# Eight stick-breaking heads placed beside the query and value tiles, and three orders of VectorE instructions changed, in a sixteen-sublayer network on one core

## The reference, cut to what matters

```python
def _swiglu(x, w_gu, w_down):                       # ffn: x + 0.5 * _swiglu(rms_norm(x))
    g, u = jnp.split(x @ w_gu, 2, axis=-1)
    return (silu(g) * u) @ w_down

def _mla_mixer(h, ...):                             # latent attention, 16 heads
    c = h @ w_in                                    # 768 query latents, 256 key-value latents, 32 rotary
    q = (rms_norm(c_q) @ w_uq); kv = (rms_norm(c_kv) @ w_ukv)
    k = concat(k_nope, k_rope); q = rms_norm(q); k = rms_norm(k)   # per head, then rotary embedding
    return softmax_attention(q, k, v) @ w_out

def rg_lru_block(x, ...):                           # linear recurrence, width 1024
    y_br = gelu(y part of x @ w_in); x_br = causal_depthwise_conv(x part)
    gates = sigmoid(x_br @ w_gates + b_gates)       # gate_i, gate_r, block by block
    a = exp(-8 * gate_r * softplus(-a_param)); u = sqrt(1 - a * a) * gate_i * x_br
    h[t] = a[t] * h[t - 1] + u[t]
    return (h * y_br) @ w_out + b_out

def stick_breaking_attention(q, k, v):              # 8 heads of 128, causal
    z = q @ k.T * 128 ** -0.5
    log_1m = where(k_pos < q_pos, log_sigmoid(-z), 0)
    suffix = reverse_cumsum(log_1m) - log_1m        # along the keys
    w = where(k_pos < q_pos, exp(log_sigmoid(z) + suffix), 0)
    return w @ v
```

## Time and profile before

| | |
|---|---|
| runs of the kernel before | 2902.45 us median (2902.28 to 2902.95, 3 runs) |
| the profiled execution's own time | 2902.22 us |
| its span, first to last instruction | 2900.4 us |
| granted TensorE clock over the span | 0.993 of full speed |
| TensorE busy | 97% of the span |
| VectorE, ScalarE, GpSimd busy | 67%, 50%, 3% |
| stick-breaking sublayer | about 2557.5 to 2685.3 us of the span |

### The profile page before, as it was taken

One profiled execution on the slowest core, in us unless ns is written; L12 is line 12 of the kernel. 1 busy time (PEld: TensorE's weight loads), 2 busy tenths in 40 slices (PEclk: granted clock), 3 DMA queues, 4 the chain that ended last, 5 costly groups with the idle time before them and its releaser, 6 DMA issues.

```text
span 2900.4 us, 47103 instructions
## 1 busy us (share of the span) xinstructions
PE 2809.0 (97%) x19844; PEld 2616.1 (90%) x19844; DVE 1955.2 (67%) x2547; ACT 1439.2 (50%) x1970; POOL 96.0 (3%) x147
## 2 busy tenths in 40 slices
PE   8999989999998999999999999999999999998998
PEld 8999979999996999998889999998899889987997
DVE  5757876565665656557655665588665778756877
ACT  5445554444456444445644444555544644445543
POOL 0000000000012000001100000000000100000000
PEclk9999999999999999999999999999999999999999
DMA  7654436676551665653345566443565456553563
GB/s 229 218 160 146 124 117 196 189 210 188 156 173 59 204 190 179 190 176 92 107 153 183 181 189 186 150 144 103 165 184 183 146 180 201 191 169 100 171 212 104
DMA packets 406278, 478.39 MB, mean 165 GB/s; under 512 B 16634, under 2 KB 332820, under 8 KB 406068
## 3 DMA queue, kind: packets, MB, share of 16 engines
q1 hardware_dynamic: 404244, 469.07, 51.5%
q0 software_dynamic: 1632, 6.25, 0.8%
q10 hardware_dynamic: 192, 0.08, 0.0%
HBM read 474.29 MB, written 1.05 MB: 164 GB/s over the span
## 4 chain that ended last, share of the span: by engine, by line
PE 87%; DVE 7%; ACT 3%; issue 2%; POOL 0%; DMA 0%; ACTq 0%; POOLq 0%; DVEq 0%
PE Wk L709 17%; PE Wk L711 17%; PE Wk L710 17%; PE Y L709 10%; PE Y L710 9%; PE Y L711 9%; DVE w_lo L1989 1%; PE Y L994 1%; DVE work L2289 1%; PE Y L818 1%; PE Wk L1084 1%; ACT w_hi L1412 1%; PE Wk L994 0%; PE Y L1068 0%; PE Wk L1068 0%
## 5 line engine op out<-in xcount | busy, mean ns | idle before, releaser
L1989 DVE TENSOR_TENSOR w_lo<-ring,w_hi 128x1024 fp32r<-128x1024 f32 (+2 forms) x910 | 1071.0, 1202 | 573.3 <-ACT w_hi L1412 529.2
L709 PE MATMUL Wk<-xT_hi,w_hi 128*128 128x256 f32 x4320 | 1229.4, 285 | 7.1 <-DVE w_lo L1989 3.5
L711 PE MATMUL Wk<-xT_hi,w_lo 128*128 128x256 f32 x4320 | 1222.2, 283 | 0.0
L710 PE MATMUL Wk<-xT_lo,w_hi 128*128 128x256 f32 x4320 | 1222.1, 283 | 0.0
L1412 ACT ACTIVATE w_hi<-ring 128x1024 fp32r<-128x1024 f32 (+1 forms) x894 | 906.9, 1039 | 598.6 <-PE Wk L711 419.1
L709 PEld LDWEIGHTS Wk<-xT_hi,w_hi 128*128 128x128 f32 x4320 | 828.4, 192 | 15.6 <-issue 7.2
L710 PEld LDWEIGHTS Wk<-xT_lo,w_hi 128*128 128x128 f32 x4320 | 828.5, 192 | 4.7 <-issue 1.0
L711 PEld LDWEIGHTS Wk<-xT_hi,w_lo 128*128 128x128 f32 x4320 | 828.3, 192 | 0.0
L709 PE MATMUL Y<-w_hi,hid_hi 128*128 128x512 f32 x936 | 368.3, 393 | 6.6 <-DVE w_lo L1989 2.6
L710 PE MATMUL Y<-w_lo,hid_hi 128*128 128x512 f32 x936 | 365.8, 391 | 0.0
L711 PE MATMUL Y<-w_hi,hid_lo 128*128 128x512 f32 x936 | 364.6, 389 | 0.0
(11 more groups left out here) (302 smaller groups left out, 2714.0 us busy)
## 6 DMA issues: line engine op xcount, KB each, us to landing
ring<-in_ffn_w_gu SPq DMA_DIRECT2D x352, 512.0 KB, 4.5
ring<-in_ffn_w_down SPq DMA_DIRECT2D x224, 512.0 KB, 4.4
ring<-in_ffn_w_up SPq DMA_DIRECT2D x96, 512.0 KB, 6.1
ring<-in_hg_w_in SPq DMA_DIRECT2D x80, 512.0 KB, 3.7
ring<-in_na_w_in SPq DMA_DIRECT2D x24, 512.0 KB, 4.6
ring<-in_hg_w_out SPq DMA_DIRECT2D x16, 512.0 KB, 3.7
ring<-in_lru_w_in SPq DMA_DIRECT2D x16, 512.0 KB, 4.1
ring<-in_kv_w SPq DMA_DIRECT2D x16, 512.0 KB, 5.1
```

The lines of the kernel that those rows point to most:

```text
L709: pe.matmul(o, l_hi, r_hi, start=first, stop=False)
L710: pe.matmul(o, l_hi, r_lo, start=False, stop=False)
L711: return pe.matmul(o, l_lo, r_hi, start=False, stop=last)
L1989: ins = dve.tensor_tensor(l, r, h.bitcast(F32), ALU.subtract)
```

## The change

It has four parts, all in the order of instructions; every matrix product stays.

1. Stick-breaking: the scores of heads 0 and 1 are issued after tile 5, of head 2 after tile 6, 3 after 7, 4 after 8, 5 after 9, 6 and 7 after 10, with `logs` and `sums` in the same stage and `exps` and `masked` in the next. `st_p` has eight buffers. `values` writes to banks 0 and 1, `w_out` waits for the heads of each tile alone, and new waits (`t_sfx`, `t_w`, `p_v`) guard the shared banks and buffers.
2. First ffn: VectorE splits tile 10 before `save_parameters`.
3. Latent attention: `ahead(16, s)` ahead of `key_unit(0)` is gone (its units are split by `ahead(18, s)`), and `key_means(2 + i)` goes ahead of `ahead(21 + 2 * i, s)`.
4. Linear recurrence: `outputs(0)` and unit 17 go ahead of `scans(6)`, and `outputs(2)` ahead of `products(4)`.

```diff
+ST_HEADS_AT = {5: (0, 1), 6: (2,), 7: (3,), 8: (4,), 9: (5,), 10: (6, 7)}
-        st_p, st_pT, st_l, st_s = wc(4, ST_N), wc(2, ST_N), wc(2, ST_N), wc(2, ST_N)
+        st_p, st_pT, st_l, st_s = wc(ST_H, ST_N), wc(2, ST_N), wc(2, ST_N), wc(2, ST_N)
...
 # TensorE, stick
                 def scores(h):
+                    pe.wait_ge(p_v, v0 + 5 + h // 2)
+                    if h >= 4:
+                        pe.wait_ge(t_sfx, h - 3)
...
                 def values(h):
                     pe.wait_ge(s_turned_sb, h0 + h + 1)
-                    if h >= 2:
+                    if h < 2:
+                        pe.wait_ge(t_sfx, 5 + h)
+                    else:
                         pe.wait_ge(s_saved, s0 + h - 1)
...
-                        mm = pe.matmul(bank(4 + h % 2)[:, kk * P:T], st_v[:, kk, h * P:(h + 1) * P],
+                        mm = pe.matmul(bank(h % 2)[:, kk * P:T], st_v[:, kk, h * P:(h + 1) * P],
...
-                    if j == 8:
-                        pe.wait_ge(p_v, v0 + 8)
-                        scores(0)
-                    if 8 <= j < 11:
-                        scores(j - 7)
+                    for h in ST_HEADS_AT.get(j, ()):
+                        scores(h)
...
-                    if i + 4 < ST_H:
-                        scores(i + 4)
                     values(i)
-                w_out(s, t0 + 12)
+                pe.wait_ge(t_sfx, ST_H)
+                for j in range(2):
+                    saved(j)()
+                    t_product(*out_of(t0 + 12, j), first=j == 0)
+                last_by_tokens(s, [out_of(t0 + 12, 2), out_of(t0 + 12, 3)], [saved(2), saved(3)])
 # ScalarE, stick
                 def logs(h):
...
                     act.wait_ge(s_psum, h0 + h + 1)
+                    if h >= 2:
+                        act.wait_ge(t_sfx, h - 1)
...
-                        logs(j - 8)
-                        if j > 8:
-                            exps(j - 9)
-                turned(0)
-                for h in range(1, ST_H):
-                    if h + 3 < ST_H:
-                        logs(h + 3)
-                    if h + 2 < ST_H:
-                        exps(h + 2)
+                    for h in ST_HEADS_AT.get(j, ()):
+                        logs(h)
+                    for h in ST_HEADS_AT.get(j - 1, ()):
+                        exps(h)
+                for h in range(ST_H):
                     turned(h)
 # VectorE, first ffn
                     hidden_parts(j, h, n0, ff_silu[:, h, :], bank(2 * h + 1))
+                    if j:
+                        splits(g + 5)
                     if s == 0 and j == PARAMETERS_AT - 1:
                         save_parameters(range(1, 8), 0)
-                    if j:
-                        splits(g + 5)
 # VectorE, mla
                 rope_keys()
-                ahead(16, s)
                 key_unit(0)
...
                         keys(1 + i)
+                        key_means(2 + i)
                         ahead(21 + 2 * i, s)
-                        key_means(2 + i)
 # VectorE, lru
                 ahead(16, s)
+                outputs(0)
+                ahead(17, s)
                 scans(6)
+                outputs(2)
                 products(4)
-                ahead(17, s)
-                outputs(0)
-                outputs(2)
+                outputs(4)
                 products(6)
-                outputs(4)
                 outputs(6)
 # VectorE, stick
                 def sums(h):
                     dve.wait_ge(t_l, h + 1)
+                    if h >= 2:
+                        dve.wait_ge(t_w, h - 1)
...
-                for j in range(8, 12):
+                for j in range(5, 12):
                     splits(t0 + j + 2)
-                    sums(j - 8)
-                    if j > 8:
-                        masked(j - 9)
-                for h in range(1, ST_H + 2):
-                    if h + 3 < ST_H:
-                        sums(h + 3)
-                    if h + 2 < ST_H:
-                        masked(h + 2)
-                    if h >= 2:
-                        saved(h - 2)
+                    for h in ST_HEADS_AT.get(j, ()):
+                        sums(h)
+                    for h in ST_HEADS_AT.get(j - 1, ()):
+                        masked(h)
+                for h in range(ST_H):
+                    saved(h)
```

More of the change, by code:

```diff
@@ L936, in w_out @@
                         t_product(*out_of(t0, j), first=j == 0)
-                if by_tokens(s):
-                    last_by_tokens(s, [out_of(t0, 2), out_of(t0, 3)], [lambda: None] * 2)
-                else:
-                    last_pair(s, out_of(t0, 2), out_of(t0, 3), lambda: None)
+                last_pair(s, out_of(t0, 2), out_of(t0, 3), lambda: None)
             def hgrn(s, idx):
@@ L1336, in turned @@
                     for n in range(3):
-                        mm = pe.transpose(bank(2 + h % 2)[:, n * P:(n + 1) * P], st_p[:, h % 4, n * P:(n + 1) * P], ident)
+                        mm = pe.transpose(bank(2 + h % 2)[:, n * P:(n + 1) * P], st_p[:, h, n * P:(n + 1) * P], ident)
                     mm.then_inc(s_turned, 1)
@@ L1342, in values, with saved @@
                     pe.wait_ge(s_turned_sb, h0 + h + 1)
-                    if h >= 2:
+                    if h < 2:
+                        pe.wait_ge(t_sfx, 5 + h)
+                    else:
                         pe.wait_ge(s_saved, s0 + h - 1)
                     for kk in range(TT):
-                        mm = pe.matmul(bank(4 + h % 2)[:, kk * P:T], st_v[:, kk, h * P:(h + 1) * P],
+                        mm = pe.matmul(bank(h % 2)[:, kk * P:T], st_v[:, kk, h * P:(h + 1) * P],
                                        st_pT[:, h % 2, 2 * kk * P:(kk + 2) * P], start=(kk == 0), stop=(kk == 1))
                     mm.then_inc(s_out, 1)
+                def saved(j):
+                    return lambda: pe.wait_ge(s_saved, s0 + 2 * j + 2)
                 s_prob0 = 2 * h0
@@ L1899, in exps @@
                     act.wait_ge(t_sfx, h + 1)
-                    act.activation(st_p[:, h % 4, :], st_s[:, h % 2, :], ACT.Exp).then_inc(t_w, 1)
+                    act.activation(st_p[:, h, :], st_s[:, h % 2, :], ACT.Exp).then_inc(t_w, 1)
                 def turned(h):
@@ L2671, in masked @@
                     dve.wait_ge(t_w, h + 1)
-                    d = st_p[:, h % 4, :]
+                    d = st_p[:, h, :]
                     d = bass.AP(d.tensor, d.offset, [list(d.ap[0]), [2 * P, TT], [1, P]])
@@ L2678, in saved @@
                     dve.wait_ge(s_out, h0 + h + 1)
-                    split_out(h, 1, bank(4 + h % 2)[:, 0:T], (s_high, g0 + h + 1), s_saved)
+                    split_out(h, 1, bank(h % 2)[:, 0:T], (s_high, g0 + h + 1), s_saved)
                 for tt in range(TT):
```

## The result

| | kernel before | changed kernel | ratio (95% interval) |
|---|---|---|---|
| first measurement, 4 runs each | 2902.7 us (2902.28 to 2909.05) | 2887.13 us (2885.34 to 2887.14) | 0.9941 (0.9928 to 0.9953) |
| second | 2902.6 us (9 runs) | 2883.93 us (2882.45 to 2886.19, 5 runs) | 0.9931 (0.9918 to 0.9943) |
| third | 2903.94 us (15 runs) | 2885.43 us (2883.52 to 2887.15, 5 runs) | 0.9937 (0.9924 to 0.9950) |

The change gains 15.6, 18.7 and 18.5 us; the forecast was 20.0. One of the fifteen runs before in the third row fell in a slow state (3106.17 us) and is left out of the ratio. The fourteen times of the changed kernel have a median of 2885.4 us, 2.9 above the forecast and inside its range. The profile of the first measurement took 2887.14 us, with a span of 2885.1 us.

The account below looks back on a forecast made before the run. TensorE, busy 2809.0 of 2900.4 us, was taken as the bound, so only its idle time and half clock could be won. Terms 12.9 + 2.55 + 2.4 + 2.1 = 20.0 us gave 2882.5 us, range 2878.5 to 2888.5.

Parts of the forecast that it names:

- Stick-breaking: Stick-breaking sublayer: old end of tile 11 to `w_out` takes 12.5 us against 25.4, gain 12.9 us.
- Product stages: Stick-breaking, end of tile 5 to end of tile 11: 39.8 us without a TensorE gap; VectorE and ScalarE keep up.
- Tail: Stick-breaking, from tile 11 to `w_out`: 2.1 + 7.6 + 0.2 us at full clock, 9.5 to 10 us expected.
- The turn: Stick-breaking tail: one transpose group and one `values` on TensorE, 0.38 + 0.66 us, 1.04 us a turn.
- the ends 5.9 and 13.6: Bounds of the stick-breaking gain: 5.9 us with the tail wholly at half clock, 13.6 if small delays are not seen.
- rival B: Stick-breaking tail: TensorE drops to half clock, 7.0 us back, 2889.5 us; chance 0.10.
- First ffn: First ffn: TensorE's 2.6 us wait for the first split of tile 10 goes; gain 2.55 us, bounds 1.2 and 2.6.
- Latent attention: Latent attention: the 2.9 us key-copy wait goes, about 3 us appears at `key_squares(1)`; gain 2.4 us, bounds 0 and 5.
- Linear recurrence: Linear recurrence: a 0.7 us wait replaces 2.85 us before `w_out`; gain 2.1 us, bounds 0.5 and 4.5.
- C: Latent attention and linear recurrence: reordered queues give their waits back one step later, 4.5 us, 2887; chance 0.12.
- E: Stick-breaking stages 5 to 10: ScalarE and VectorE wait for each other; slower than before, about 2907; chance 0.03.
- F: Stick-breaking: stalls of the product stages eat the heads' gain, about 2902; chance 0.03.

Follow-up runs that it names:

- experiment 7: Changed kernel with TensorE's order in latent attention altered, queries ahead of the key squares: 2887.06 us, against 2883.93 for the changed kernel.
- experiment 6: Changed kernel with useless products filling TensorE's waits in the last pair of hg heads, both hg sublayers: 2881.07 us, against 2883.93 for the changed kernel.
- experiment 11: Changed kernel with the edits of experiment 6, experiment 8 and experiment 10 together: 2879.94 us, against 2885.43 for the changed kernel.
- experiment 12: The changed kernel measured a third time, text unchanged: 2885.43 us, five runs from 2883.52 to 2887.15.
- experiment 10: Changed kernel with linear recurrence's eight bias products run four and four, the last branch between them: 2885.77 us, against 2885.43 for the changed kernel.
- experiment 8: Changed kernel with linear recurrence's output-weight splits of steps 18 and 19 made earlier on VectorE: 2885.58 us, against 2883.93 for the changed kernel.
- experiment 2: Kernel before with only the stick-breaking part of the change: 2889.29 us, ratio 0.9949.
- experiment 9: Kernel before with only the latent attention part of the change: 2902.49 us, ratio 0.9999.

## Why the prediction was right, point by point

**Stick-breaking, forecast 12.9 us, measured 13.4** (from 127.84 to 114.47 us; 114.44 to 114.48 in all nine kernels that have it). Of it, 7.9 us are idle time and about 5 are the half of 10.3 us that ran at half clock before. Product stages: 39.8 us forecast, 39.8 read, with VectorE busy 29.9 us (32.2 forecast) and ScalarE 30.3 (31.2). Tail: 9.9 us forecast, 9.44 read. The turn takes 0.99 us, not 1.04. TensorE waits for the copy of tile 11 for 0.69 us as forecast, and for the first copy of the weights' transposes for only 0.33. No gap is over 0.7 us, and the clock stays at 1.00. The choice between the ends 5.9 and 13.6 went by the short gaps of the earlier trace rows, and rightly: rival B did not occur in any profile. What the argument had not seen is where the old tail's half clock began, at waits of 2.79 and 3.26 us; that the clock stays up over gaps of 0.69 and 0.33 us fits it.

**First ffn, forecast 2.55, measured 2.65.** The wait went, and the copies run under the matmuls of tile 10. What the term left out is on the other side: the wait that it removes is in other executions followed by half clock (196.56 and 197.73 us with the old order), so that the median gain may be larger: 3.3 us when tried alone, with an interval (0.9 to 6.4 us) too wide to show it.

**Latent attention, forecast 2.4, measured 0.7 in the whole kernel and 2.3 alone.** `key_unit(0)` ended at 1351.9 and the 2.9 us wait went. The wait ahead of `key_squares(1)`, about 3 us forecast, is 2.13 us, and that ahead of `key_squares(2)`, forecast without a size, 1.33. The eight splits took 3.84 us where 4.7 was the sum, because GpSimd's copies took 4.00 us and not 5.29 and had ended when the splits began, so nothing was left of the 1.4 us of overlap. The key copies took 1.51 us a pair under GpSimd's copies (1350.42, 1353.01) and 1.51 us without them (1358.43): they lost nothing, as the sum has it. This part of the step is right. At `query_squares(1)` TensorE waits 1.83 us for the query means, and is through at 1383.93 us in place of 1385.64, though it began the sublayer 0.25 us later: 2.0 us won up to there. Behind that the term failed: behind the 0.79 us wait at 1413.50 the clock stood at half for 6.8 us in place of 3.4, which with what follows took 1.2 us back. Over the ten profiles with the new order (without that of experiment 7) the sublayer is 162.83 to 165.18 us, mean 164.4; over the three with the old order 165.17 to 165.89, mean 165.6: 1.3 us. The term was too large by about 1 us. It counted the half clock behind a wait that it removed, and no more half clock behind the waits that remain.

**Linear recurrence, forecast 2.1, measured 1.8** (from 86.41 us to between 84.56 and 84.68). The wait is 0.99 to 1.02 us in place of the 0.7 us of the sum. The clock fell ahead of it, during the bias products, as the earlier trace rows showed; no wait is needed for it in any of the twelve profiles with eight bias products in a row.

**The untouched sublayers, forecast 0.** Here stands the rest. The first hg sublayer is 2.5 and 3.0 us longer in two of three profiled executions and not longer in the third; the second hg sublayer 0.4 us longer in all, which is within what it takes in the experiments that leave it alone (202.09 to 205.58 us). Why the changed kernel took the longer form in two of three, while seven of the eight other kernels with this sublayer's text unchanged took 201.9 to 203.0 us (the eighth 205.1), is not settled: the kernel before was profiled once, and three executions aren't enough for a frequency. One rival stays open: the longer form stands in three of the seven such profiles with the shorter first ffn and in none of the five in which that ffn is not shorter, too few to tell a link from chance. That the stretches at half clock hang on the waits of the last pair is shown (experiments 6 and 11); that the length is picked by the execution and not the program is shown by three profiles of one text with the same waits, and times of one text spread over 3.6 us within one set (experiment 12); what picks it is not shown.

**The sum of all clock.** In the profiled executions of the changed kernel, the time less half of the us read at half clock is 2887.14 - 18.8 = 2868.3, 2883.93 - 15.5 = 2868.4 and 2887.15 - 18.8 = 2868.4. All of the 3.2 us between them is thus clock. Against the kernel before, the first execution has 10.3 us less at half clock in the heads' tail and 3.4 less in linear recurrence, 6.8 more in the first hg, 3.4 more in the second, and 1.7 more at the very end, where TensorE has finished and they cost nothing. So of the 6.8 us that the change won in clock (half of 13.7), the untouched hg sublayers took 5.1 back in that execution, which is more than the 4.9 us between forecast and profile.

Of the rivals, C is the nearest in time for the first profile (2887), but for the wrong reason: VectorE's two reordered queues fell short of their terms by 1.4 us by the means (2.0 in the first profile), not 4.5. E and F are excluded by the gapless 39.8 us.

## What to carry to other kernels

When TensorE is near its limit, give each wait that remains its price with the clock behind it, from 0 to 2.8 us here for one wait of 2.56 us, and look at it in several executions: one profile can't tell a term of 3 us from a draw. If an idle time can't be removed, fill it with products that nobody reads, as long as they end before the awaited operand comes: it cost nothing here, and a filled hg sublayer is 1.5 us shorter on average than one without (201.8 against 203.35). Moving TensorE's own order when another engine's sum is the bound only moves the wait, or makes it longer (experiments 7 and 10). And before a stretch at half clock is put down to an edit, look for the same stretch in kernels without the edit: experiment 8 has it, and so do three kernels that lack its edit.

## What the runs showed of the hardware

- The granted clock falls to half while TensorE is busy without a gap, behind eight matmuls that multiply by a single row (1 x 128 weights, 512 columns): 0.58 from 2304 to 2312 us, in experiment 8, at 8.00 us busy of 8.00, and in all twelve profiles that have the eight in a row. Four of them with 128-row products between did so in one execution (experiment 11) and not in another (experiment 10).
- One and the same text with the same wait of 2.56 us ran on at 1.00, or with 3.4, or with 6.8 us at half clock (kernel before, experiments 2 and 9): 194.97, 196.56 and 197.73 us for one sublayer.
- Four of VectorE's splits, which read two tensors, took 4.50 us beside GpSimd's copies before, and the four copies 5.29 us. With the key copies in the splits' place, which read one tensor from PSUM, GpSimd's copies took 4.00 us and the key copies 1.51 us a pair, as without GpSimd. The eight splits behind them took 3.84 us, 0.48 us each, which is the undisturbed rate of the earlier trace rows (1.97 for four).
